# A bias table's 128-fold copy made from DRAM rows in the first MLP instead of from on-chip rows in the first mixer, and a new order of the first loads

## The chip, the cores and the metric

One of the eight cores of a Trainium2 chip runs the whole kernel; the other seven are not used. The metric is the device time of one execution in microseconds (us), as the median of several runs of the same program. Lower is better. Beside these runs one execution was recorded by the hardware profiler, and every row below is from that one.

## The reference

The model is a stack of six layers over 256 tokens of width 1024, in float32, batch 1. Cut to what matters here:

```
x = x                                    # 256 x 1024
for i in 0..3:                           # "first block"
    h = rms_norm(x, norm_mix[i])
    m = retention | conformer | stick_breaking | retention   (h)
    x = x + m
    x = x + (relu(rms_norm(x, norm_ffn[i]) @ w1[i]) ** 2) @ w2[i]      # 1024 -> 4096 -> 1024
x = rms_norm(x, final_norm)
for layer in 0..1:                       # "second block"
    x = hybrid_layer(x, ..., rel_bias)   # short conv + pooling + windowed attention, then a gated MLP
return rms_norm(x, g_final)
```

Windowed attention adds to each score a bias that depends on the head and on key position minus query position: `bias = rel_bias[t5_bucket(rel)]`, 16 heads, `rel_bias` is 32 x 16. So for each head there is one vector over the relative position, and every query row uses the same vector shifted by one.

All weights together are some 400 MB of float32, each read once. With 256 tokens this gives TensorE enough work per byte to be the bound, since each product is taken as three float32r matmuls (high x high, high x low, low x high parts).

## The kernel before

**Units.** All weights lie in one DRAM tensor in the order of use, cut into units of 2 MB (some of 1 MB). A unit is two pieces of 128 x 2048 floats. For each piece: SP (SyncE) issues one DMA into `raw[u % 2]` (L495, `load`, called in loops from `loads` and `mlp`), ScalarE copies it to float32r as the high part `w_hi` (L1113), VectorE subtracts to get the low part `w_lo` (L1512), and TensorE multiplies (L691, L692, L693). There are two slots of each. The load of unit u waits until the low part of unit u-2 is made; the split of unit u waits until TensorE is through with the same piece of unit u-2. `ahead(v)` on ScalarE and VectorE emits the splits up to unit v at that place of the engine's order.

**Order.** Every engine has its own instruction list, written out by hand, and they meet at semaphores only. Nothing is scheduled by a planner. Layer 1 is a retention mixer of 16 units, then an MLP of 16 units (`mlp_walk`), then the conformer, and so on. `row` and `Fori` only fold repeated units into hardware loops.

**The first norm (`norm`, `norm_half`).** It runs in two halves of 128 tokens. For each half ScalarE squares x and sums (L1180), VectorE adds epsilon and inverts (L1576, L1577), ScalarE takes the root (L1183), VectorE scales (L1633), TensorE transposes (L728), VectorE multiplies by the norm's gain, which lies in `cols` (L1639), and ScalarE and VectorE make high and low parts (L1162, L1565). Before the first unit can start, all this must be done for half 0 and both parts of the unit's first piece must be there. At the start SP issues the loads of x half 0, the identity matrix (for transposes), `cols` (the column tables), x half 1, and then the weights. GpSimd (POOL) issues at the same time the tables of the retention mixer (rope, gains, decay), `rel_bias` and the one-hot bucket table. VectorE and TensorE wait for `loaded` to reach 32, which is identity and `cols` both.

**The bias table.** In the first mixer TensorE makes the 16 vectors by one small product (L832), VectorE copies them from PSUM to `B_VEC`, 16 partitions of 512 floats. GpSimd then writes them to a DRAM tensor `scratch` of 16 x 128 x 512 floats (4 MB), each row 128 times. It does so in four DMAs of 1 MB (`store_bias`, L558), each of four heads, thus from four partitions of `B_VEC`, one after each head's rows of the group norm (`ret_gn_w`, `ret_gn_b`, fetched by L537). Much later the two hybrid layers read `scratch` with a row length of 511, which gives each query row its shifted vector. After the first mixer GpSimd fetches a row, zeroes, waits for all four stores (`stored` 64), since its next work overwrites `B_VEC`, and then makes the conformer's diagonal matrices (L583), which TensorE reads in the second layer.

Of the kernel before, what the change touches and what calls it, by code (L numbers as in the profile page):

```python
# [24 lines left out]
F32 = mybir.dt.float32  # L25
F32R = mybir.dt.float32r
ALU = mybir.AluOpType
ACT = mybir.ActivationFunctionType
AX = mybir.AxisListType

P = 128
# [10 lines left out]
N_HEADS, N_KV, HEAD_DIM, WINDOW = 16, 4, 64, 128  # L42
# [269 lines left out]
    last()  # L312

def build_program(nc, stream, columns, x_in, rows, tables, rel_bias, scratch, out):
    col_at, n_cols = column_layout()
    widths = unit_widths()
    n_units = len(widths)
# [3 lines left out]
    with ctx:  # L322
# [3 lines left out]
        def sem(name):  # L326
            return ctx.enter_context(nc.semaphore(name))
# [66 lines left out]
        sca = sem("sca")  # L394
        x_in_place = [sem(f"x_in_place{a}") for a in range(2)]
        loaded = sem("loaded")
        table = sem("table")
        gn_rows = sem("gn_rows")
        bias_in = [sem(f"bias_in{i}") for i in range(2)]
# [21 lines left out]
        def tiles(ap, t=SEQ):  # L421
            return ap.rearrange("p (k t) -> p k t", t=t)
# [57 lines left out]
        @block.sync  # L480
        def _(sp):
            S = Place()

            def load():

                slot, n = S.u % 2, widths[S.u] // 2
                if S.u >= 2:
                    sp.wait_ge(lo_done, S.at(2 * (S.u - 1), "u", 2))
                for piece in range(2):
                    rows_n = P * n // D  # L490
                    row = S.at(S.row, "row")
                    src = stream[row:row + rows_n, :] if S.it is None else stream[bass.ds(row, rows_n), :]
                    if n > D:
                        src = src.rearrange("(p a) n -> p (a n)", p=P)
                    sp.dma_start(raw[slot][:, place_of(S.u, piece)], src).then_inc(arrived[slot][piece], 16)  # L495
                    S.row += rows_n
                S.u += 1

            def loads(n):

                def body():
                    load()
                    load()
                if S.u == 0:
                    body()
                    n -= 2
                repeat(sp, S, n // 2, {"u": 2, "row": 2 * P * UNIT // D}, body)
                if n % 2:
                    load()

            def mlp(chunks, width):
                def step(first):
                    load()
                    load()
                mlp_walk(sp, S, chunks, {"u": 4, "row": 2 * P * (UNIT + width) // D}, load, step, load)

            sp.dma_start(x[:, 0, :], x_in[0:P, :]).then_inc(x_in_place[0], 16)
            sp.dma_start(ident[:], tables["identity"]).then_inc(loaded, 16)
            sp.dma_start(cols[:], columns).then_inc(loaded, 16)
            sp.dma_start(x[:, 1, :], x_in[P:SEQ, :]).then_inc(x_in_place[1], 16)  # L520
            for mixer_units in (16, 6, 8, 16):
                loads(mixer_units)
                mlp(FFN1_CHUNKS, UNIT)
            for layer in range(2):
                loads(14)
                load()
                loads(9)
                mlp(FFN2_CHUNKS, UNIT // 2)
            assert S.row == stream.shape[0] and S.u == n_units
# [3 lines left out]
        def _(pool):  # L533
            S = Place()

            def fetch(dst, src, done=table):
                pool.dma_start(dst, src).then_inc(done, 16)  # L537

            def row_of(src):
                return src.partition_broadcast(P)  # L540
# [6 lines left out]
            def region_free():  # L547

                pool.wait_ge(released, S.due("released"))
# [1 line left out]
            zero(B_REL)  # L551
            zero(B_REL[32:33, :], 1.0)

            def store_bias(part):

                hs = slice(4 * part, 4 * part + 4)
                pool.dma_start(scratch[hs], B_VEC[hs, :].unsqueeze(1).broadcast_to([4, P, 512])).then_inc(stored, 16)  # L558

            def retention(j):  # L560
                if j:
                    region_free()
                fetch(work[:, 5632:6144], tables["rope"])
                fetch(R_GAIN[:, 0, :], row_of(rows["ret_q_norm"][j, :]))
                fetch(R_GAIN[:, 1, :], row_of(rows["ret_k_norm"][j, :]))
                fetch(work[:, 4096:5632], tables["decay"])
                if j == 0:
                    fetch(B_REL[0:32, 0:N_HEADS], rel_bias)
                    fetch(B_HOT, tables["bucket_hot"])
                for h in range(RET_HEADS):  # L570
                    if h:
                        region_free()
                    fetch(R_GN[:, 0, :], row_of(rows["ret_gn_w"][j, RET_DV * h:RET_DV * (h + 1)]), gn_rows)
                    fetch(R_GN[:, 1, :], row_of(rows["ret_gn_b"][j, RET_DV * h:RET_DV * (h + 1)]), gn_rows)
                    if j == 0:
                        if h == 0:
                            pool.wait_ge(bias_vec, 1)
                        store_bias(h)

            def diagonals(n):  # L580

# [17 lines left out]
            fetch(C_B, row_of(rows["conv_pw2_b"][0, :]))  # L599
            zero(C_U[:, :, 0:TAPS - 1])  # L600
            zero(C_MEAN, 1.0 / D)
            pool.wait_ge(stored, 64)
            pool.wait_ge(loaded, 32)
            diagonals(0)
            diagonals(1)
            split_low(CONV_FIRST + 3)
# [12 lines left out]
            retention(1)  # L619
            region_free()  # L620
            fetch(ROW, row_of(rows["final_norm"]), row_in)
            flat = scratch.rearrange("h t r -> h (t r)")
            for layer in range(2):
                if layer:
# [22 lines left out]
            for a in range(2):  # L647
                pool.wait_ge(x_ready, x_signals - 2 + 2 * a)
                pool.dma_start(out[P * a:P * (a + 1), :], xs[:, a, :]).then_inc(stored, 16)
            pool.wait_ge(stored, 96)  # L650

        @block.tensor
        def _(pe):
# [426 lines left out]
                    await_chunks(1)  # L1081
                    unit_r(act_hi, act_lo, 4 * i, 4, i == 0, i == 1)

            pe.wait_ge(loaded, 32)
            first_half()
            for i, mixer in enumerate((retention, conformer, stick_breaking, retention)):
                if i in (0, 3):
# [15 lines left out]
        def _(act):  # L1103
# [81 lines left out]
            def norm(first=False, row=False):  # L1185

                if not first:
                    ahead(S.u)
                for a in range(2):
                    if row:  # L1190
                        norm_half(a)
                    norm_half(a, first)
                    if a == 1:
                        ahead(S.u)
                    use(False)
                    S.v += 1
                    act.wait_ge(value_ready, S.v)
                    for g in range(2):
                        if g == 1:
                            await_drained(S.p - 1)  # L1200
                        round_chunk(act_hi[:, four(g), P * a:P * (a + 1)],
                                    tiles(val[:, g, 512 * a:512 * (a + 1)], P))

            def mlp1():
                def make(ahead_too):
# [190 lines left out]
            def hybrid(layer):  # L1396
# [86 lines left out]
                    round_chunk(act_hi[:, four(i), :], tiles(H_MERGED[:, i, :]))  # L1483
                S.u += 2

            for i, mixer in enumerate((retention, conformer, stick_breaking, retention)):
                norm(first=i == 0)
                mixer()
                norm()
                mlp1()  # L1490
# [12 lines left out]
        def _(dve):  # L1503
# [94 lines left out]
            def inverse_rms(a):  # L1598
                dve.wait_ge(ss_ready, S.due("ss_ready"))
                inverse(rinv[:, a:a + 1], ss[:, a:a + 1])  # L1600
# [9 lines left out]
            def norm(name, add=True, row=False):  # L1610

                if add:
                    ahead(S.u)

                def low(a, g):
                    ts_, cs = slice(P * a, P * (a + 1)), slice(512 * a, 512 * (a + 1))
                    rest_chunk(act_hi[:, four(g), ts_], act_lo[:, four(g), ts_], tiles(val[:, g, cs], P))

                for a in range(2):  # L1620
                    if a == 1:
                        low(0, 0)
                    if add:
                        residual_half(a)
                    elif a == 1:
                        dve.wait_ge(x_in_place[1], 16)
                    if row:
                        row_norm_half(a, x)
                    if a == 1:
                        low(0, 1)  # L1630
                    inverse_rms(a)
                    await_roots()
                    ts(xs[:, a, :], x[:, a, :], rstd[:, a:a + 1], None, ALU.mult).then_inc(xs_ready, 1)  # L1633
                    if not add and a == 1:
                        ahead(S.u)
                    o, done = fetch_pair()
                    S.v += 1
                    for g in range(2):
                        tt(tiles(val[:, g, 512 * a:512 * (a + 1)], P), tiles(o[:, 512 * g:512 * (g + 1)], P),  # L1639
                           by_tile(name, 4 * g, 4, P), ALU.mult).then_inc(done if g else value_ready, 1)  # L1640
                low(1, 0)
                low(1, 1)
# [443 lines left out]
                    rest_chunk(act_hi[:, four(i), :], act_lo[:, four(i), :], tiles(H_MERGED[:, i, :]))  # L2086
                S.u += 2

            dve.wait_ge(loaded, 32)
            dve.wait_ge(x_in_place[0], 16)  # L2090
            for i, mixer in enumerate((retention, conformer, stick_breaking, retention)):
                norm(f"norm_mix{i}", add=i > 0)
# [42 lines left out]
```

## Time and profile before

| | us |
|---|---|
| median of 3 runs | 2608.0 |
| lowest, highest | 2607.62, 2610.07 |
| profiled execution, first to last instruction (span) | 2603.1 |
| TensorE busy in it | 2426.9 (93%) |
| VectorE, ScalarE, GpSimd busy | 1531.0 (59%), 1139.3 (44%), 184.8 (7%) |
| share of the chain that ended last: TensorE, VectorE, DMA, ScalarE | 78%, 11%, 5%, 3% |

The profiled execution is read from its first to its last instruction. Its own time is not listed among the runs; the median of the runs is 4.9 us longer than its span, which is launch and end. TensorE's busy share is an average over a long, even part and a few stretches where it stands still. The first mixer lies between 20 and 251 us of the span, the first MLP between 251 and 444 us, and the second retention mixer, which has the same units and none of the bias table's work, between 1126 and 1335 us.

### The profile page before, as it was taken

Reading aid. Unit: us, or ns where it says so; the run is one execution under the profiler, and the core shown is the slowest. Engines: PE = TensorE matmul, PEld = TensorE weight load, DVE = VectorE, ACT = ScalarE, POOL = GpSimd, SP = SyncE. Lnnn points to the kernel's source line nnn. Section 1 sums busy time; section 2 is a strip of 40 time slices with the busy share of each in tenths; the row PEclk is TensorE's granted clock in tenths of the full one; section 3 lists DMA queues with packets and bytes.
Section 4 is the critical chain, followed back from the end, with each engine's and each line's share of the span. In section 5 each row is a group of like instructions: output and inputs, shape, how many; then the busy total and the mean of one; then the engine's idle time right before and its main releaser. Section 6 shows DMA issues by size and latency. Waiting matters only on the chain.

```text
span 2603.1 us, 35299 instructions
## 1 busy us (share of the span) xinstructions
PE 2426.9 (93%) x14772; PEld 2165.5 (83%) x14772; DVE 1531.0 (59%) x1476; ACT 1139.3 (44%) x1119; POOL 184.8 (7%) x198
## 2 busy tenths in 40 slices
PE   7988899859999899999999999997999999979998
PEld 5766898848997789977879979996899899968997
DVE  6655555986556664476664566457654564485544
ACT  5433444224445843354443444354444433453443
POOL 0000810611000000000000000002000000020000
PEclk9999999989999999999999999998999999989999
DMA  6565444213444245434454435351444444522443
GB/s 237 161 178 162 182 181 181 98 65 130 181 184 175 82 158 194 193 151 181 178 199 194 193 130 194 147 205 57 176 166 189 185 184 169 187 105 114 169 179 128
DMA packets 68402, 424.35 MB, mean 163 GB/s; under 512 B 10832, under 2 KB 11120, under 8 KB 22464
## 3 DMA queue, kind: packets, MB, share of 16 engines
q1 hardware_dynamic: 58752, 399.83, 40.0%
q0 software_dynamic: 9536, 22.87, 3.8%
q8 instruction: 87, 1.43, 0.2%
q14 instruction: 27, 0.22, 0.0%
HBM read 417.40 MB, written 5.24 MB: 162 GB/s over the span
## 4 chain that ended last, share of the span: by engine, by line
PE 78%; DVE 11%; DMA 5%; ACT 3%; issue 2%; SPq 0%; POOL 0%; DVEq 0%; ACTq 0%; POOLq 0%
PE pair L691 16%; PE pair L693 16%; PE pair L692 16%; PE acc L691 8%; PE acc L692 8%; PE acc L693 8%; DMA raw<-weights 3%; DVE work L1812 2%; DVE work L1792 2%; DMA work<-ret_gn_b 1%; DVE w_lo L1512 1%; PE pair L728 1%; PE pair L1056 1%; ACT work L1180 1%; DVE work L2036 1%
## 5 line engine op out<-in xcount | busy, mean ns | idle before, releaser
L1512 DVE TENSOR_TENSOR w_lo<-raw,w_hi 128x2048 fp32r<-128x2048 f32 (+1 forms) x394 | 837.8, 2159 | 312.6 <-ACT w_hi L1113 311.8
L1113 ACT ACTIVATE w_hi<-raw 128x2048 fp32r<-128x2048 f32 (+1 forms) x404 | 713.7, 1805 | 214.7 <-PE acc L693 133.4
L691 PE MATMUL pair<-act_hi,w_hi 128*128 128x256 f32 x2496 | 708.7, 284 | 3.1 <-DVE w_lo L1512 3.1
L693 PE MATMUL pair<-act_hi,w_lo 128*128 128x256 f32 x2496 | 706.3, 283 | 0.0
L692 PE MATMUL pair<-act_lo,w_hi 128*128 128x256 f32 x2496 | 706.3, 283 | 0.0
L691 PEld LDWEIGHTS pair<-act_hi,w_hi 128*128 128x128 f32 x2496 | 478.9, 192 | 6.1 <-issue 3.8
L692 PEld LDWEIGHTS pair<-act_lo,w_hi 128*128 128x128 f32 x2496 | 478.9, 192 | 2.3
L693 PEld LDWEIGHTS pair<-act_hi,w_lo 128*128 128x128 f32 x2496 | 478.9, 192 | 0.0
L691 PE MATMUL acc<-w_hi,hid_hi 128*128 128x512 f32 x848 | 336.2, 397 | 10.8 <-DVE hid_lo L1565 10.8
L692 PE MATMUL acc<-w_lo,hid_hi 128*128 128x512 f32 x848 | 332.4, 392 | 0.0
L693 PE MATMUL acc<-w_hi,hid_lo 128*128 128x512 f32 x848 | 331.9, 391 | 0.0
L691 PE MATMUL pair<-w_hi,act_hi 128*128 128x512 f32 (+1 forms) x576 | 226.2, 393 | 13.1 <-DVE w_lo L1512 7.9
L693 PE MATMUL pair<-w_hi,act_lo 128*128 128x512 f32 (+1 forms) x576 | 222.3, 386 | 0.0
L692 PE MATMUL pair<-w_lo,act_hi 128*128 128x512 f32 (+1 forms) x576 | 222.3, 386 | 0.0
L691 PEld LDWEIGHTS acc<-w_hi,hid_hi 128*128 128x128 f32 x848 | 160.7, 190 | 44.8 <-DVE hid_lo L1565 11.6
L693 PEld LDWEIGHTS acc<-w_hi,hid_lo 128*128 128x128 f32 x848 | 160.3, 189 | 34.0
L692 PEld LDWEIGHTS acc<-w_lo,hid_hi 128*128 128x128 f32 x848 | 160.7, 190 | 32.8 <-issue 1.4
L1654 DVE TENSOR_TENSOR val<-gate 128x1024 f32<-128x1024 f32 x32 | 39.2, 1225 | 207.7 <-ACT gate L1207 207.7
L691 PEld LDWEIGHTS pair<-w_hi,act_hi 128*128 128x128 f32 x576 | 109.3, 190 | 39.0 <-issue 11.5
L1207 ACT ACTIVATE gate<-pair 128x1024 f32<-128x1024 f32 x32 | 32.8, 1026 | 243.2 <-PE pair L693 237.2
L693 PEld LDWEIGHTS pair<-w_hi,act_lo 128*128 128x128 f32 x576 | 109.1, 189 | 21.9
L692 PEld LDWEIGHTS pair<-w_lo,act_hi 128*128 128x128 f32 x576 | 109.2, 190 | 21.2 <-issue 0.7
(209 smaller groups left out, 2683.7 us busy)
## 6 DMA issues: line engine op xcount, KB each, us to landing
raw<-weights SPq DMA_DIRECT2D x356, 1024.0 KB, 6.7
raw<-weights SPq DMA_DIRECT2D x48, 512.0 KB, 6.4
work<-bias_scratch POOLq DMA_DIRECT2D x32, 192.0 KB, 3.4
bias_scratch<-work POOLq DMA_DIRECT2D x4, 1024.0 KB, 48.4
work<-ret_gn_w POOLq DMA_DIRECT2D x8, 256.0 KB, 5.0
work<-ret_gn_b POOLq DMA_DIRECT2D x8, 256.0 KB, 12.7
work<-table_pool POOLq DMA_DIRECT2D x2, 1024.0 KB, 5.6
work<-table_decay POOLq DMA_DIRECT2D x2, 768.0 KB, 8.9
```

The lines of the kernel that those rows point to most:

```text
L691: mm(o, a_hi, b_hi, start=start, stop=False)
L692: mm(o, a_hi, b_lo, start=False, stop=False)
L693: return mm(o, a_lo, b_hi, start=False, stop=stop)
L728: last = tr(o[:, P * k:P * (k + 1)], xs[:, a, P * k:P * (k + 1)], ident[:])
L1056: last = mm(o[:, 512 * i:512 * i + SEQ], H_V[:, s, P * (j // 4):P * (j // 4) + P], H_PT[:, j % 2, i, s, :], start=s == 0, stop=s == 1)
L1113: run(w_hi[slot][:, part], raw[slot][:, part], ACT.Copy).then_inc(hi_done, 1)
L1180: run(xs[:, a, :], x[:, a, :], ACT.Square, scale=D ** -0.5, accum_out=ss[:, a:a + 1]).then_inc(ss_ready, 1)
L1207: run(gate[:, slot, :], o[:], ACT.Relu).then_inc(done, 1)
L1512: tt(w_lo[slot][:, part], raw[slot][:, part], w_hi[slot][:, part].bitcast(F32), ALU.subtract).then_inc(lo_done, 1)
L1654: tt(val[:, S.c % 2, :], gate[:, slot, :], gate[:, slot, :], ALU.mult).then_inc(value_ready, 1)
L1792: ins = stt(C_Y[:, k, :], C_U[:, k, m:m + SEQ], colv("dw_w", KT * m + k), C_Y[:, k, :], ALU.mult, ALU.add)
L1812: ins = stt(dst, src, w, dst, ALU.mult, ALU.add)
```

## The change

The bias vectors are stored once, as 16 rows, to a new DRAM tensor `bias_rows` (one DMA of 32 KB). The four DMAs that make 128 copies read those rows from DRAM, and GpSimd issues them together once the first mixer is over. GpSimd waits only for the small store before that, and for all four copies only before the hybrid layers. The loads at the start get another order: the first unit of weights is issued piece by piece around x half 1, GpSimd's tables wait until the first unit has landed (`arrived[0][1]`), the wait for `cols` moves to the instruction that reads it, ScalarE's root table is loaded ahead by a dummy root, and on ScalarE and VectorE the split of the first unit stands ahead of the second half's norm. Note that `load()` issues both pieces of a unit; so the order on SP is x half 0, identity, `cols`, unit 0, x half 1, unit 1.

```diff
@@ SP
-                if S.u == 0:
-                    body()
-                    n -= 2
...
             sp.dma_start(x[:, 0, :], x_in[0:P, :]).then_inc(x_in_place[0], 16)
             sp.dma_start(ident[:], tables["identity"]).then_inc(loaded, 16)
-            sp.dma_start(cols[:], columns).then_inc(loaded, 16)
+            sp.dma_start(cols[:], columns).then_inc(cols_in, 16)
+            load()
             sp.dma_start(x[:, 1, :], x_in[P:SEQ, :]).then_inc(x_in_place[1], 16)
-            for mixer_units in (16, 6, 8, 16):
+            load()
+            for mixer_units in (14, 6, 8, 16):
@@ GpSimd
-            def store_bias(part):
-                hs = slice(4 * part, 4 * part + 4)
-                pool.dma_start(scratch[hs], B_VEC[hs, :].unsqueeze(1).broadcast_to([4, P, 512])).then_inc(stored, 16)
             def retention(j):
                 if j:
                     region_free()
+                else:
+                    pool.wait_ge(arrived[0][1], 16)
                 fetch(work[:, 5632:6144], tables["rope"])
...
-                    if j == 0:
-                        if h == 0:
-                            pool.wait_ge(bias_vec, 1)
-                        store_bias(h)
+                    if j == 0 and h == 0:
+                        pool.wait_ge(bias_vec, 1)
+                        pool.dma_start(bias_rows, B_VEC[0:N_HEADS, :]).then_inc(stored, 16)
...
             zero(C_MEAN, 1.0 / D)
-            pool.wait_ge(stored, 64)
-            pool.wait_ge(loaded, 32)
+            pool.wait_ge(stored, 16)
+            for part in range(4):
+                hs = slice(4 * part, 4 * part + 4)
+                pool.dma_start(scratch[hs], bias_rows[hs].unsqueeze(1).broadcast_to([4, P, 512])).then_inc(stored, 16)
+            pool.wait_ge(loaded, 16)
+            pool.wait_ge(cols_in, 16)
             diagonals(0)
...
             fetch(ROW, row_of(rows["final_norm"]), row_in)
+            pool.wait_ge(stored, 80)
@@ TensorE
-            pe.wait_ge(loaded, 32)
+            pe.wait_ge(loaded, 16)
             first_half()
@@ ScalarE, norm
                     norm_half(a, first)
-                    if a == 1:
+                    if a == 1 and not first:
                         ahead(S.u)
...
+                    if a == 0 and first:
+                        ahead(S.u)
@@ ScalarE, start
+            act.wait_ge(root_primed, 1)
+            run(small[:, 127:128], small[:, 126:127], ACT.Sqrt)
@@ VectorE, norm
-                    elif a == 1:
-                        dve.wait_ge(x_in_place[1], 16)
...
                     if a == 1:
                         low(0, 1)
+                        if not add:
+                            ahead(S.u)
+                            dve.wait_ge(x_in_place[1], 16)
                     inverse_rms(a)
                     await_roots()
                     ts(xs[:, a, :], x[:, a, :], rstd[:, a:a + 1], None, ALU.mult).then_inc(xs_ready, 1)
-                    if not add and a == 1:
-                        ahead(S.u)
                     o, done = fetch_pair()
+                    if not add and a == 0:
+                        dve.wait_ge(cols_in, 16)
@@ VectorE, start
-            dve.wait_ge(loaded, 32)
+            nc.vector.memset(small[:, 126:127], 1.0).then_inc(root_primed, 1)
             dve.wait_ge(x_in_place[0], 16)
```

## Rows read from the trace of the kernel before

**Rows 1.** Page: the span, and the shares of the chain that ended last.

```profile
span 2603.1 us, 35299 instructions
...
PE 78%; DVE 11%; DMA 5%; ACT 3%; issue 2%; SPq 0%; POOL 0%; DVEq 0%; ACTq 0%; POOLq 0%
```

**Rows 2.** Busy time by stretch: mixers, MLPs, an even part, a part at half clock.

```profile
core 0: us, PE busy (x) PEld busy (x) DVE busy (x) ACT busy (x) POOL busy (x), PEclk, DMA share, GB/s
85.23:251.29 166.06, 145.89 (x619) 115.89 (x619) 90.39 (x86) 64.12 (x48) 6.65 (x9) 0.94 0.61 169
1191.46:1335.12 143.66, 139.77 (x619) 111.51 (x619) 89.75 (x85) 63.50 (x48) 3.21 (x6) 1.00 0.48 177
251.29:444.14 192.85, 185.44 (x1132) 165.79 (x1130) 101.12 (x65) 80.88 (x59) 63.47 (x65) 0.98 0.51 190
608.94:792.19 183.25, 182.32 (x1131) 163.92 (x1130) 100.56 (x65) 80.68 (x59) 6.55 (x8) 1.00 0.48 184
...
340.00:420.00 80.00, 80.00 (x524) 73.61 (x523) 40.52 (x21) 30.55 (x20) 0.00 (x0) 1.00 0.51 197
158.20:168.40 10.20, 5.33 (x15) 4.39 (x16) 5.61 (x5) 5.62 (x4) 0.00 (x0) 0.50 0.46 137
```

**Rows 3.** TensorE's waits, 0 to 300 us: total, times, longest.

```profile
PE pair L854 <- ACT work L1263: 12.3, 3, 8.6
...
PE acc L691 <- DVE hid_lo L1565: 8.3, 2, 5.9
```

**Rows 4.** Chain of waits, 85 to 300 us: start, length, what.

```profile
93.61 31.46 DMA raw<-weights
...
130.05 30.12 DMA raw<-weights
...
249.26 28.42 DMA raw<-weights
```

**Rows 5.** Landing of the weights' DMAs, issues of 260 to 440 us.

```profile
DMA to landing us min/median/max: 4.7/6.6/8.9
```

**Rows 6.** Page, DMA issues: count, size of each, median us to landing.

```profile
bias_scratch<-work POOLq DMA_DIRECT2D x4, 1024.0 KB, 48.4
```

**Rows 7.** Timeline of ScalarE, VectorE and TensorE, 0 to 21 us, in parts.

```profile
4.08 1.06 ACT L1180 ACTIVATE work<-x 128x1024 f32<-128x1024 f32 x1 [2.04 <-DMA x<-x_in]
5.05 0.19 ACT L1180 ACTIVATION_READ_ACCUMULATOR work<-x 128x1 f32 x1
5.25 1.28 ACT L1183 ACT_TABLE_LOAD   x1
...
8.68 0.15 DVE L1576 TENSOR_SCALAR small<-small 128x1 f32<-128x1 f32 x1 [8.68 <-DMA cols<-columns]
...
12.90 1.22 ACT L1162 ACTIVATE act_hi<-val 128x512 fp32r<-128x512 f32 x2 [3.63 <-DVE val L1639]
...
15.69 1.89 ACT L1113 ACTIVATE w_hi<-raw 128x2048 fp32r<-128x2048 f32 x1
17.62 2.29 DVE L1512 TENSOR_TENSOR w_lo<-raw,w_hi 128x2048 fp32r<-128x2048 f32 x1 [1.05 <-ACT w_hi L1113]
...
20.06 0.77 PE L691 MATMUL pair<-w_hi,act_hi 128*128 128x512 f32 x1 [7.92 <-DVE w_lo L1512]
```

**Rows 8.** DMA from 82.5 to 85 us: the first store alone.

```profile
DMA packets 795, 0.07 MB, mean 27 GB/s; under 512 B 780, under 2 KB 780, under 8 KB 795
```

**Rows 9.** DMA from 2594 to 2597 us: one output store; packets, MB, engine share.

```profile
q0 software_dynamic: 144, 0.52, 43.1%
```

**Rows 10.** GpSimd: the last store's issue and the diagonals behind the wait.

```profile
226.04 1.12 POOL L558 DMA_DIRECT2D bias_scratch<-work  x1 [32.75 <-issue]
...
274.33 62.41 POOL L583 TENSOR_SCALAR work<-ident,cols 128x128 f32<-128x128 f32 x62 [11.59 <-issue]
```

**Rows 11.** Waits of ScalarE, 608 to 792 us: its splits wait on TensorE.

```profile
ACT w_hi L1113 <- PE acc L693: 24.6, 7, 3.5
```

**Rows 12.** DMA from 18 to 23 us: all kinds together.

```profile
DMA packets 315, 1.90 MB, mean 380 GB/s; under 512 B 48, under 2 KB 48, under 8 KB 118
```

More of the change, by code:

```diff
@@ L312, in mlp_walk, with build_program @@
     last()
-def build_program(nc, stream, columns, x_in, rows, tables, rel_bias, scratch, out):
+def build_program(nc, stream, columns, x_in, rows, tables, rel_bias, bias_rows, scratch, out):
     col_at, n_cols = column_layout()
@@ L396, in build_program @@
         loaded = sem("loaded")
+        cols_in = sem("cols_in")
+        root_primed = sem("root_primed")
         table = sem("table")
@@ L649, in _ @@
                 pool.dma_start(out[P * a:P * (a + 1), :], xs[:, a, :]).then_inc(stored, 16)
-            pool.wait_ge(stored, 96)
+            pool.wait_ge(stored, 112)
         @block.tensor
@@ L2128 @@
     tables = {k: given("table_" + k, v) for k, v in constant_tables().items()}
+    bias_rows = nc.dram_tensor("bias_rows", (N_HEADS, 512), F32).ap()
     scratch = nc.dram_tensor("bias_scratch", (N_HEADS, P, 512), F32).ap()
@@ L2131 @@
     build_program(nc, given("weights", lay_out_weights(a)), given("columns", lay_out_columns(a)),
-                  given("x_in", a["x"][0]), rows, tables, given("rel_bias", a["rel_bias_2"]), scratch, out)
+                  given("x_in", a["x"][0]), rows, tables, given("rel_bias", a["rel_bias_2"]), bias_rows, scratch,
+                  out)
     result = run_bass_kernel_spmd(nc, [arrays], core_ids=[0])
```

## The prediction

> **What bounds the kernel now.** I read the page first. The chain that ended last is TensorE for 78% [rows 1], so a change pays only where TensorE stands still or runs at the lower clock. The page has no such place by name, so I read the first layer by stretches against later layers with the same units. Retention mixer 0 from its first attention product (85.23 us) to the next norm takes 166.06 us; the same stretch of retention mixer 1, with the same 619 matmuls, takes 143.66 us [rows 2]. The first MLP takes 192.85 us, the second, with the same 1132 matmuls, 183.25 us [rows 2]. So 22.4 us and 9.6 us are lost there to something that later layers don't have. TensorE's waits show it standing for ScalarE and VectorE results, 12.3 us and 8.3 us, with single waits of 8.6 and 5.9 us [rows 3]. Their causes stand in the chain of waits: behind them are loads of weights that need 28.4 to 31.5 us to land [rows 4], where 6.6 us is usual [rows 5]. Each of these lies beside one store of the bias table, which takes 48.4 us [rows 6]. After such a wait the clock is at its lower level, 1.2 GHz, for some 10 us (158.2 to 168.4 us, granted clock 0.50 [rows 2]). At the opening TensorE's first product of a unit starts at 20.06 us, released by the low part of the weights [rows 7].
>
> **Why a store is slow.** Alone on the queues it moves 27 GB/s [rows 8]. One output store from 128 partitions moves 0.52 MB in 43.1% of 16 engines for 3 us, which is 20.7 engine-us, so 25.3 GB/s for each engine [rows 9]. The store of four partitions thus gets about one engine's rate in all, while the weights on the same engines queue behind it: in the chain, four pieces of 1 MB are out at once and the last needs about 30 us, 7.5 us each, or 15.0 us for a unit. The MLP wants a unit each 183.25 / 16 = 11.45 us. That gives the stall: 48.4 x (1 - 11.45 / 15.0) = 11.5 us at most per store, less what is buffered; measured are (22.4 + 9.6) / 4 = 8.0 us, lower clock included.
>
> **The change, part by part.**
>
> *Four stores leave mixer 0.* Only one store of 32 KB remains, a thirty-second of one of the four. The stretch becomes that of mixer 1: 166.06 - 143.66 = 22.4 us gained. Nothing else differs after 85 us; the group norm's rows are fetched in both. Bounds: 20 (a late landing remains) to 22.4.
>
> *The first MLP loses its share of the fourth store,* issued at 226.04 and over by 274.33, where GpSimd goes on behind its wait for it [rows 10]: 192.85 - 183.25 = 9.6 us gained.
>
> *Four copies DRAM to DRAM enter the first MLP.* The trace has none such, so I bound it. From below: 4.2 MB at 25.3 GB/s per engine [rows 9] over 16 engines is 10.4 us of DMA time. The DMA share there is 0.51 at 197 GB/s [rows 2], so half of the engines' time is free, and the copies are through in some 20 us. A weight packet of 8 KB takes 8.2 / (197 / 0.51 / 16) = 0.34 us of an engine, a copy's 4 KB 0.16 us; if an engine takes one of each in turn, a piece (8 packets per engine) needs 4.0 us and a unit 8.0 us, below the 11.45 wanted. It makes no difference to this whether the four copies use four engines each or all use the same four. ScalarE's splits wait on TensorE in an MLP, not on DMAs [rows 11], so a landing some us later is hidden. From above: each copy costs what a store costs now or more (rivals below). Below nothing is excluded, since the work is added. I take 0.5 us, near the lower end, since the nearest rows with a spread source or target [rows 9] show full rate and only the four-partition source shows 27 GB/s.
>
> *GpSimd.* Its four issues of 1.12 us [rows 10] come ahead of the diagonals, and the wait for the stores goes. Now the diagonals start at 274.33 and take 62.4 us [rows 10], and they are read after 444 us. They may be 100 us late at no cost. The wait for the copies now stands before the hybrid layers, two mixers and three MLPs on.
>
> *The opening,* step by step. ScalarE squares half 0 from 4.08 and has the sum at 5.24 [rows 7]. VectorE goes on only at 8.68, when `cols` has landed. With that wait moved it starts at 5.27, so 3.41 us earlier. The root's table load (5.25 to 6.53) was hidden by that wait; now it would cost 0.9 us, and the dummy root moves it ahead of 4.08, in an idle time of 2.04 us that ended with x. `cols` itself, needed 3.5 us after the start of L1576, lands at 8.65 or earlier, as the tables of GpSimd no longer share the engines: just in time. So the first high part of the activations moves from 12.90 to 9.49 and the pair of them ends at 10.71. Then ScalarE splits the weights at once, instead of after half 1's square and root: from 15.69 to 10.73, gain 4.96. VectorE's low part follows 1.93 us later and TensorE 2.44 us after that [rows 7]: 15.10 instead of 20.06. Condition: the first piece is there at 10.73. It is behind `cols` (8.65 at the latest) and takes 1.05 MB / 380 GB/s [rows 12] = 2.8 us, so 11.4 at the latest; earlier if `cols` is. Half 1's chain moves behind the splits, but ends near 19 us, and TensorE turns it only after 15 products, near 21 us. The tables that now wait for the first unit (about 12.5 us) are 1.5 MB of some 4.5 MB queued then, all landed by 12.5 + 4.5 / 0.38 = 24.3; VectorE wants them near 25. The first products run at the lower clock; after a stall that lasts up to 10 us [rows 2], and if it lasts a few us longer here than it did, up to 1.9 us go. I take 4.5 us; bounds 2.6 and 5.0.
>
> **Sum.** 22.4 + 9.6 + 4.5 - 0.5 = 36.0 us. The span goes from 2603.1 to 2567.1; the runs' median lies 4.9 us above the span, so 2608.0 becomes 2572.0. All later layers shift as they are, since their chains start at the end of the first MLP.
>
> **The rivals.**
>
> *R1, the copies stay slow but run side by side.* If it is the 2 KB rows or the writes into DRAM that set the rate, and not the source's partitions, each copy still takes 48 us, and the four together load all 16 engines for that time. One stretch of 11.5 us of stall, plus some 2 us at the lower clock: 13.5 in place of 0.5, 2585. For it: the rows of the store don't separate source from target. Against it: the 27 GB/s is just one engine's rate. The Trainium skill (DMA: Bandwidth & Descriptors, "Rules for kernel authors") says that an outermost dimension of size c below 16 confines a DMA to at most c engines, and the copies still have 4 outermost, so it speaks for narrow copies. With narrow copies at full engine rate the sum stays; with slow ones it is R1 or R2, and no row before shows which.
>
> *R2, slower than before.* The copies stay slow and queue one after another on the same four engines: 4 x 48.4 = 194 us, the whole MLP. Then every unit takes 15.0 instead of 11.45 us: 16 x 3.55 = 57 us lost against 36.5 gained, 2628. It decides from 11.45 + 36.5 / 16 = 13.7 us per unit on. The weights' 30 us landings [rows 4] speak for it, the wide stores' rate [rows 9] against it.
>
> *R3, the stalls only move:* each copy costs 8.0 us in the MLP as each store does now, 32 in all, and only the opening stays: 2603.5.
>
> *R4, the opening gives nothing,* since the first weights or `cols` come late under the saturated queues (380 GB/s [rows 12]): 2576.5.
>
> **Chances.** Forecast 0.72, R1 0.12, R4 0.09, R3 0.04, R2 0.03. What can be told from no change is about 0.2%, 5.2 us. Faster: 0.72 + 0.12 + 0.09 = 0.93; within it R3, 0.04; slower R2, 0.03. The range reaches from 2568 us (all terms at their upper bound and a us or two of clock) to 2585, R1's value, where about 1 in 10 is left above.
>
> **What would show it.** The mixer from its first attention product to the next norm takes 143 to 146 us, and no weights' load needs over 15 us. The first MLP takes 183 to 185 us; each copy lands in under 30 us, and the clock stays at 1.00 between 30 us and the end of this MLP. The first product of a unit starts near 15 us. The forecast is wrong if TensorE waits for `hid_lo` or a split in the first MLP with a weights' load behind it (R1 to R3), or if L1113 waits for a DMA near 11 us (R4).

## The result and the profile after

The changed kernel takes 2569.93 us (median of 4 runs, 2568.25 to 2571.21) against 2607.81 us (4 runs, 2606.49 to 2610.07) beside it: 37.9 us less, ratio 0.9852, 95% interval 0.984 to 0.9864. The forecast was 2572.0 us, with a range of 2568 to 2585 and a chance of 0.93 that the kernel gets faster. In the profiled executions the span fell by 34.1 us only, from 2603.1 to 2569.0; the difference is explained below.

The page of the changed kernel: the span, the shares of the chain that ended last, the landing of the copies.

```profile
span 2569.0 us, 35304 instructions
...
PE 86%; DVE 10%; ACT 3%; issue 1%; DMA 0%; POOL 0%; DVEq 0%; ACTq 0%
...
bias_scratch<-bias_rows POOLq DMA_DIRECT2D x4, 1024.0 KB, 22.7
```

DMA had 5% of the chain [rows 1] and has 0% now. By stretches (length, busy time of each engine, granted clock, DMA share, GB/s): head, mixer 0, mixer 1, first MLP, second MLP.

```profile
15.16:79.55 64.39, 62.45 (x283) 50.71 (x283) 52.21 (x67) 36.22 (x61) 2.28 (x5) 1.00 0.53 207
79.55:223.98 144.43, 141.26 (x619) 112.66 (x619) 89.92 (x86) 63.48 (x48) 3.23 (x6) 0.99 0.48 180
1155.70:1300.13 144.43, 141.26 (x619) 112.62 (x619) 89.85 (x85) 63.45 (x48) 3.22 (x6) 0.99 0.48 178
223.98:407.20 183.22, 182.29 (x1131) 163.91 (x1129) 100.96 (x65) 80.69 (x59) 62.61 (x69) 1.00 0.56 212
574.32:757.53 183.21, 182.25 (x1131) 163.91 (x1130) 100.55 (x65) 80.69 (x59) 6.60 (x8) 1.00 0.48 184
```

These answer [rows 2]. Mixer 0 went from 166.06 to 144.43 us and is now as long as mixer 1 to a hundredth. The first MLP went from 192.85 to 183.22 us, the length of every other, although 4 MB of copies (DMA at 212 instead of 184 GB/s) run in it.

The opening, ScalarE, VectorE and TensorE, answers [rows 7]: start, length, what, and what ended the idle time before.

```profile
0.77 1.28 ACT L1491 ACT_TABLE_LOAD   x1 [0.77 <-PEq L2121]
4.17 1.06 ACT L1182 ACTIVATE work<-x 128x1024 f32<-128x1024 f32 x1 [1.91 <-DMA x<-x_in]
5.83 0.20 ACT L1185 ACTIVATE small<-small 128x1 f32<-128x1 f32 x1 [0.51 <-DVE small L1583]
9.66 1.23 ACT L1164 ACTIVATE act_hi<-val 128x512 fp32r<-128x512 f32 x2 [3.63 <-DVE val L1646]
10.80 3.69 ACT L1115 ACTIVATE w_hi<-raw 128x2048 fp32r<-128x2048 f32 x2
...
5.44 0.15 DVE L1582 TENSOR_SCALAR small<-small 128x1 f32<-128x1 f32 x1 [4.54 <-ACT work L1182]
...
15.16 0.77 PE L693 MATMUL pair<-w_hi,act_hi 128*128 128x512 f32 x1 [6.26 <-DVE w_lo L1518]
```

The first product starts at 15.16 instead of 20.06 us. ScalarE takes both pieces of the first unit with no wait for a load: the first piece lands at 9.36 us, where it landed at 14.84 us before.

GpSimd's timeline, which answers [rows 10]:

```profile
75.51 0.51 POOL L575 DMA_DIRECT2D bias_rows<-work  x1 [58.58 <-DVE work L1730]
...
236.13 1.12 POOL L602 DMA_DIRECT2D bias_scratch<-bias_rows  x1 [0.73 <-POOL work L545]
259.68 1.10 POOL L602 DMA_DIRECT2D bias_scratch<-bias_rows  x1 [22.43 <-issue]
283.52 1.09 POOL L602 DMA_DIRECT2D bias_scratch<-bias_rows  x1 [22.74 <-issue]
306.05 1.08 POOL L602 DMA_DIRECT2D bias_scratch<-bias_rows  x1 [21.43 <-issue]
307.25 57.17 POOL L580 TENSOR_SCALAR work<-ident,cols 128x128 f32<-128x128 f32 x62
```

Here the forecast's picture was off: the copies don't go out together. Each is issued 0.3 to 0.4 us after the one before has landed, so they fill 92 us and not 20, and the diagonals start 33 us later than before, in spite of a mixer that ends 27 us earlier. They still end 43 us ahead of the end of the MLP. The trace of before showed the same: its stores were issued at 81.22, 127.57, 176.96 and 226.04 us, the last three 0.35 to 0.42 us after the one before had landed. The sign in [rows 10] is the 32.75 us that GpSimd stood idle before the last store, with nothing that the profile shows to wait for. So a store was under way almost without a break from 81 to 274 us.

One stretch shows how copy and weights share an engine. From 254 to 258 us DMA's share is 0.27, some four of 16 engines, so only the engines that the copy uses are at work:

```profile
254.00:258.00 4.00, 4.00 (x20) 3.30 (x19) 3.59 (x3) 4.00 (x4) 0.00 (x0) 1.00 0.27 109
```

109 GB/s over 4.3 engines is 25 GB/s for each, the rate of the output store [rows 9]. In this stretch the trace has 34 copy packets of 4 KB, of 0.159 us, and 34 weight packets of 8 KB, of 0.309 us: one of each in turn, as the sum assumed (0.16 and 0.34 us). The slowest weight load took 12.6 us (min/median/max 4.7/6.7/12.6), and no split waited for one.

### The profile page after: what moved, and what is told of

It is laid out like the page before. It is cut to its first block, busy times and chain, and to the rows that moved or that the text cites. A ratio compares the mean times of both kernels' runs of the same rounds, so it can differ in the third digit from the quotient of the medians.

```text
span 2569.0 us, 35304 instructions
## 1 busy us (share of the span) xinstructions
PE 2421.5 (94%) x14772; PEld 2162.4 (84%) x14772; DVE 1530.4 (60%) x1477; ACT 1137.2 (44%) x1119; POOL 180.5 (7%) x199
## 4 chain that ended last, share of the span: by engine, by line
PE 86%; DVE 10%; ACT 3%; issue 1%; DMA 0%; POOL 0%; DVEq 0%; ACTq 0%
PE pair L693 18%; PE pair L695 17%; PE pair L694 17%; PE acc L693 9%; PE acc L694 9%; PE acc L695 9%; DVE work L1819 2%; DVE work L1799 2%; PE pair L730 1%; PE pair L1058 1%; PE acc L1037 1%; ACT work L1182 1%; PE pair L1000 1%; DVE work L2043 1%; ACT act_hi L1164 0%
## 5 line engine op out<-in xcount | busy, mean ns | idle before, releaser
L695 PEld LDWEIGHTS acc<-w_hi,hid_lo 128*128 128x128 f32 x848 | 160.0, 189 | 34.1
## 6 DMA issues: line engine op xcount, KB each, us to landing
bias_scratch<-bias_rows POOLq DMA_DIRECT2D x4, 1024.0 KB, 22.7
```

The costliest lines, as they stand in the source:

```text
L695: return mm(o, a_lo, b_hi, start=False, stop=stop)
```

## The experiments

All times are against the kernel before on the same chip. Stretches are those of [rows 2]: the mixer from its first attention product to the next norm, then the first MLP.

### The opening alone, and the copies alone

`e_open_only` has the diff's edits of the opening and the four old stores; `e_copies_only` has the diff's copies and the old opening (its first product comes at 20.65 us).

> Kernel before with the new opening alone; the four stores stay in mixer 0. Main theory (the parts add up): first product of a unit near 15.2 us instead of 20.06, the mixer stretch from the first attention product to the next norm stays near 166 us and the first MLP near 192.9 us, time about 4.9 us below before. Rival (the stalls beside the stores absorb a head start, since they end when weights land): the mixer stretch grows by the 4.9 us, time within 1 us of before.

> Kernel before with the bias rows stored once and the four DRAM-to-DRAM copies in the first MLP; the opening as before. Main theory: first product at 20 us, mixer stretch 144 us, first MLP 183 us, time 31 to 33 us below before; the copies follow one another and land in 22 to 24 us each. Rival (the copies only fit because the new opening gives a lead): first MLP above 186 us.

The opening alone takes 2603.69 us (11 runs) against 2607.58 (15 runs), ratio 0.9982 (0.9973 to 0.9991). Mixer and MLP, of `e_open_only` and then of `e_copies_only`:

```profile
79.71:247.95 168.24, 148.54 (x619) 117.75 (x619) 90.42 (x86) 64.12 (x48) 6.64 (x9) 0.92 0.59 168
247.95:439.45 191.50, 184.12 (x1131) 164.90 (x1130) 101.38 (x65) 80.89 (x59) 66.12 (x65) 0.99 0.51 191
```

```profile
84.91:229.34 144.43, 141.27 (x618) 112.64 (x619) 89.95 (x86) 63.49 (x48) 3.23 (x6) 0.99 0.49 180
229.34:412.56 183.22, 182.28 (x1131) 163.91 (x1130) 101.07 (x65) 80.67 (x59) 62.74 (x69) 1.00 0.56 212
```

The first product of `e_open_only` comes at 15.16 us, and 4.7 of the 4.9 us are there still at the end of the first MLP (439.45 against 444.14). The mixer is 2.2 us longer, the MLP 1.4 shorter. So the stalls do not absorb the head start, though the mixer takes 2.2 us of it for a while. The copies alone give 2575.96 us, ratio 0.9879 (0.9864 to 0.9894), 31.6 us less, with both stretches as in the changed kernel. The parts add up: 31.6 + 3.9 = 35.5 us against 37.9 for both, within the spread of the runs.

### Source or place

Two kernels with the old opening separate what the change does in one step. `e_dram_in_mixer` takes the copies from DRAM rows but at the old places:

```diff
-                    if j == 0 and h == 0:
-                        pool.wait_ge(bias_vec, 1)
-                        pool.dma_start(bias_rows, B_VEC[0:N_HEADS, :]).then_inc(stored, 16)
+                    if j == 0:
+                        if h == 0:
+                            ...
+                            pool.wait_ge(stored, 16)
+                        hs = slice(4 * h, 4 * h + 4)
+                        pool.dma_start(scratch[hs], bias_rows[hs].unsqueeze(1).broadcast_to([4, P, 512])).then_inc(stored, 16)
```

> Opening as before; the rows go once to DRAM and the four 1 MB copies from DRAM are issued at the old four places in mixer 0. Main theory (the source counts: four partitions give one engine's rate, DRAM rows don't): mixer stretch 144 to 147 us, first MLP 183 to 184 us, copies land in 15 to 24 us, time 30 to 33 us below before. Rival (the place counts: the mixer has no slack for a 1 MB copy, the MLP has): mixer stretch 152 us or more, time at most 22 us below before.

`e_sbuf_in_mlp` keeps the on-chip source but issues at the new place:

```diff
-                pool.dma_start(scratch[hs], bias_rows[hs].unsqueeze(1).broadcast_to([4, P, 512])).then_inc(stored, 16)
+                pool.dma_start(scratch[hs], B_VEC[hs, :].unsqueeze(1).broadcast_to([4, P, 512])).then_inc(stored, 16)
...
             diagonals(0)
+            pool.wait_ge(stored, 64)
```

> Opening as before; the four stores keep their on-chip source of four partitions but are issued in the first MLP, one after another. GpSimd must wait for them before the second set of diagonals, so these come late and the conformer may wait for them; the verdict is read from the MLP. Main theory (source counts): mixer stretch 144 us, and the first MLP has a stall beside every store: 192.9 - 183.2 is what most of one store costs, so four of them give 200 to 240 us (15.0 us per unit over all 16 units would be 240). Rival (place counts): first MLP 183 to 187 us.

Mixer and MLP of `e_dram_in_mixer`, then of `e_sbuf_in_mlp`, and three loads of the latter from its chain of waits (start, length):

```profile
87.30:230.99 143.69, 139.79 (x619) 111.53 (x619) 89.84 (x86) 63.46 (x48) 6.66 (x9) 1.00 0.58 206
230.99:414.21 183.22, 182.28 (x1132) 163.93 (x1130) 101.35 (x65) 80.69 (x59) 73.84 (x65) 1.00 0.49 193
```

```profile
85.59:229.25 143.66, 139.75 (x619) 111.52 (x619) 89.86 (x86) 63.49 (x48) 3.20 (x6) 1.00 0.48 179
229.25:452.32 223.07, 193.01 (x1132) 171.18 (x1130) 101.19 (x65) 82.05 (x59) 48.00 (x51) 0.92 0.57 170
```

```profile
253.17 31.46 DMA raw<-weights
289.67 27.66 DMA raw<-weights
...
353.25 31.70 DMA raw<-weights
```

DRAM rows in the mixer cost nothing: 143.69 us, copies land in 22.9 us, 2576.41 us in all, ratio 0.9877 (0.9862 to 0.9893), the same as `e_copies_only`. The on-chip rows in the MLP cost 223.07 - 183.22 = 39.9 us there. TensorE stands for them in two kinds of wait for a split, and the rest is mostly its clock: busy time is 193.01 us instead of 182.28 for the same products, at a granted clock of 0.92.

```profile
PE acc L689 <- DVE w_lo L1510: 16.8, 3, 9.7
PE pair L689 <- DVE w_lo L1510: 11.5, 2, 9.2
```

So 28.3 us are waits and 10.7 us the lower clock. The kernel takes 2615.68 us against 2608.44, ratio 1.0033 (1.0023 to 1.0044), slower than before. So the source gives the whole gain and the place none. With the old source, moving to the MLP alone is a loss.

### The width of the copy

`e_wide_sbuf` changes only which part of the table one store writes. Place, source tensor and bytes stay as before:

```diff
-                hs = slice(4 * part, 4 * part + 4)
-                pool.dma_start(scratch[hs], B_VEC[hs, :].unsqueeze(1).broadcast_to([4, P, 512])).then_inc(stored, 16)
+                ts_ = slice(32 * part, 32 * part + 32)
+                pool.dma_start(scratch[:, ts_, :], B_VEC[0:N_HEADS, :].unsqueeze(1).broadcast_to([N_HEADS, 32, 512])).then_inc(stored, 16)
```

> Kernel before, stores at the old places in mixer 0 and still from on-chip rows, but each store writes 32 copies of all 16 rows, so its source is 16 partitions instead of 4. Opening as before. If the source's partitions set the rate (four ports of 27 GB/s, by the Trainium skill, SBUF - State Buffer, Door 1): a store lands in 12 to 14 us instead of 48, mixer stretch 144 to 148 us, time 28 to 33 us below before. Rival (an on-chip source to DRAM in 2 KB rows is slow as such, 27 GB/s for the DMA): landing stays near 48 us and, with all 16 engines behind it, the mixer stretch is 166 us or more.

Mixer and MLP, and the landing of its four stores:

```profile
84.54:228.25 143.71, 139.81 (x619) 111.51 (x619) 89.86 (x86) 63.49 (x48) 5.13 (x9) 1.00 0.67 207
228.25:411.47 183.22, 182.28 (x1132) 163.92 (x1130) 101.31 (x65) 80.69 (x59) 73.59 (x65) 1.00 0.48 190
```

```profile
DMA to landing us min/median/max: 12.0/12.7/13.3
```

A store from 16 partitions lands in 12.7 us, and one from four in 48.4 [rows 6]. The time is 2576.71 us, ratio 0.9882 (0.9867 to 0.9897): the copies' whole gain, with no detour through DRAM. The Trainium skill (SBUF — State Buffer, "Door 1: The DMA port swizzle") gives 104 GB/s as measured for partitions 0 to 15 and 1 MiB. By that figure a store would take 10.1 us, an estimate; the 12.7 us here, beside weights' loads, are somewhat above it.

This kernel changes two things at once, the partitions of the source and the number of engines, and its time alone doesn't separate them. The DRAM copies do in part: with four outermost they land in 22.7 us, so four engines alone don't make a store last 48.4 us. The packets settle the rest. In `e_sbuf_in_mlp` a store's packet of 4 KB takes 0.34 us when two of them are under way at once, 0.48 us with three and 0.62 us with four (medians), while a DRAM copy's packet takes 0.16 us with any number from one to four. So the four engines of a store share one rate of some 4 x 4.1 / 0.62 = 26 GB/s, and it isn't that each partition has a fixed low rate of its own, which would give 0.6 us at any number. With 16 packets from 16 partitions under way (`e_wide_sbuf`) one takes 0.61 us, which is 107 GB/s in all, four times as much. The same times say why weights are late. Averaged over what is under way, a store's packet takes 0.51 us in `e_sbuf_in_mlp` and 0.60 us in the kernel before (84 to 106 and 229 to 260 us). An engine that takes one packet of each kind in turn, as was counted for the copies, would then need 0.82 to 0.91 us for every weight packet, thus 6.6 to 7.3 us for the eight packets of a piece, near the 7.5 that the forecast read from the landings.

`e_wide_dram` does the same to the changed kernel's copies (`bias_rows.unsqueeze(1).broadcast_to([N_HEADS, 32, 512])`), and `e_half_copies` cuts each into two of 64 copies, still four heads each.

> Changed kernel, but each of the four copies writes 32 copies of all 16 rows, so the outermost dimension is 16 and not 4. By the Trainium skill (DMA: Bandwidth & Descriptors, Rules for kernel authors) a copy then uses 16 engines instead of 4: it lands in 4 to 8 us instead of 22.7, and GpSimd issues the next one that much sooner, so the diagonals start some 60 us earlier. Time the same as the changed kernel within 1 us, since the first MLP is already at 183.2. Rival (GpSimd's issue gaps of 22 us have another cause, and the DRAM rows' rate sets the landing): landing stays above 15 us. Second rival: wide copies hit all weights' engines at once and the first MLP goes above 185 us.

> Changed kernel, but each of the four copies is cut in two of 64 copies each, still with 4 outermost. In the changed kernel GpSimd issued a copy only when the one before had landed (gaps of 22 us), in the wide version all four without a gap. If the issue waits for room on the few engines that a narrow copy uses (the same four each time), then the first two or more halves go out at once, and the gaps that follow are about half as long, 10 to 12 us each; all eight are out near 306 us as before. Rival (GpSimd lets only one narrow copy be under way at a time, whatever its size): every half waits for the one before, eight gaps of 10 to 12 us. Second rival (they use different engines and only the number of descriptors in one DMA counts): no gaps at all, all out by 242 us. In each case the first MLP stays at 183.2 us.

GpSimd's timeline, of the wide and then of the half copies:

```profile
236.31 2.57 POOL L602 DMA_DIRECT2D bias_scratch<-bias_rows  x4 [0.31 <-POOL work L545]
239.00 69.33 POOL L580 TENSOR_SCALAR work<-ident,cols 128x128 f32<-128x128 f32 x62
```

```profile
235.98 2.65 POOL L602 DMA_DIRECT2D bias_scratch<-bias_rows  x3 [0.38 <-POOL work L545]
256.97 2.49 POOL L602 DMA_DIRECT2D bias_scratch<-bias_rows  x3 [18.34 <-issue]
278.13 1.65 POOL L602 DMA_DIRECT2D bias_scratch<-bias_rows  x2 [18.67 <-issue]
279.90 40.42 POOL L580 TENSOR_SCALAR work<-ident,cols 128x128 f32<-128x128 f32 x42
```

All four wide copies go out in 2.6 us, and the last lands at 262.3 us, so all 4 MB take 26 us from the first issue. (The four count on one semaphore, so the landings of the first three can't be told apart for certain.) The diagonals start 68 us earlier. The slowest weights' load takes 15.0 us and ScalarE waits 1.9 us for one, but TensorE does not: the MLP takes 183.23 us, and the time is 2570.79 us against 2608.44, ratio 0.9858 (0.9842 to 0.9874), as the changed kernel. I had expected each copy to land in 4 to 8 us, which overlooked that they would now share the engines with each other.

The halves go out three at a time, which is none of the three patterns I had written down: the first theory had "two or more at once" right, its gaps (18 us for 10 to 12) and its end (279 us for 306) wrong. Its premise, that narrow copies use the same four engines each time, is wrong too. From 238.5 to 243 us the trace has 4, then 8, then 12 packets of the halves under way at once, so three halves use three groups of four engines; under one copy of the changed kernel it is at most four but for some 3% of the time. A theory of room for rows on one engine therefore doesn't fit as it stood. Shown is only this: one copy of 1 MB with 4 outermost, three halves, or all four wide copies go out together, and the next group follows 0.4 us after the last of the group has landed (256.58 and 277.78 us). What limits the group stays open. The MLP takes 183.22 us again, and the time is 2569.79 us in one run.

### The opening, piece by piece

Five variants of the changed kernel, each with one thing altered. `e_tables_first` takes away GpSimd's wait for the first unit; `e_no_prime` the dummy root; `e_cols_wait` puts the wait for `cols` back ahead of the first norm; `e_late_split` puts `ahead(S.u)` back behind the second half's root and scaling; `e_piece_early` (with the wide copies) puts the first piece's split between the two activation chunks:

```diff
+                        if first and a == 0:
+                            split_piece(0, g)
+                            S.split = g
```

> Changed kernel without GpSimd's wait for the first unit, so its tables load from 1.5 us on as before. If the order of the loads carries the opening: the first piece lands after 12 us instead of near 9.4, L1115 waits for a DMA and the first product comes at 17 us or later. Rival (the first pieces land in time anyway and only the order of the engines' instructions counts): first product within 0.3 us of 15.16.

> Changed kernel without the dummy root. Main theory: the root's table loads after the sum of half 0, from about 5.3 to 6.6 us, so the root comes at 6.6 instead of 5.83 and the first product near 15.9 to 16.0 instead of 15.16. Rival (another table is loaded once anyway and the start is set by the weights): 15.16 within 0.2.

> Changed kernel, but VectorE waits for the column tables before the first norm, as before. The tables land near 6.9 us now (before: 8.65). Main theory: L1582 starts near 6.9 instead of 5.44, and the first product comes 1.3 to 1.7 us later than 15.16 (16.5 to 16.9). Rival (the weights' split is the last to be ready whatever VectorE does): 15.16 within 0.3.

> Changed kernel, but ScalarE and VectorE split the first unit after half 1's norm, as before. Main theory: half 1's square and root stand ahead of the split, so the first product comes 1.5 to 2.0 us later than 15.16 (16.7 to 17.2), or later if half 1 of x, now behind the first unit in the queue, lands after 11 us: then up to 18.6. Rival (loads alone carry the opening): 15.16 within 0.3.

> As e_wide_dram, and in the opening ScalarE and VectorE take the first piece's split between the two activation chunks of half 0. Expected: first product at 14.5 to 14.8 us instead of 15.16, 0.4 to 0.6 us less in all, which only the timeline can tell. Rival: the first piece has not landed near 10.3 us and the start stays at 15.1 or later.

TensorE's first product in `e_tables_first`, `e_no_prime`, `e_cols_wait`, `e_late_split` and `e_piece_early`, from their timelines:

```profile
15.15 0.77 PE L691 MATMUL pair<-w_hi,act_hi 128*128 128x512 f32 x1 [6.28 <-DVE w_lo L1516]
```

```profile
15.96 0.76 PE L693 MATMUL pair<-w_hi,act_hi 128*128 128x512 f32 x1 [6.26 <-DVE w_lo L1516]
```

```profile
16.65 0.77 PE L693 MATMUL pair<-w_hi,act_hi 128*128 128x512 f32 x1 [6.26 <-DVE w_lo L1518]
```

```profile
12.82 1.06 ACT L1182 ACTIVATE work<-x 128x1024 f32<-128x1024 f32 x1 [1.86 <-DMA x<-x_in]
...
18.93 0.76 PE L693 MATMUL pair<-w_hi,act_hi 128*128 128x512 f32 x1 [9.96 <-DVE w_lo L1516]
```

```profile
14.71 0.76 PE L693 MATMUL pair<-w_hi,act_hi 128*128 128x512 f32 x1 [5.67 <-DVE w_lo L1519]
```

So at the first product the opening's parts are worth 0.8 us (dummy root), 1.5 us (wait for `cols`), 3.8 us (split ahead of half 1), and nothing for the tables' delay. The last was a miss: with the tables under way the first piece landed at 10.75 us instead of 9.36, just in time for the split at 10.77; only the second piece and half 1 came late (ScalarE waited 2.39 us for the piece). TensorE's first attention product came at 80.04 us, between the 79.55 of the changed kernel and the 80.88 of `e_wide_dram`, which has the same opening, so no loss shows there either. The other half of the new load order, the first unit ahead of half 1 of x, was not tried by itself. It can't be free: with both halves of the old order the first piece landed at 14.84 us, 4.1 us after the 10.7 at which ScalarE now takes it. One run each gave 2571.40 us without the tables' delay, 2570.76 without the dummy root, 2571.19 with the wait for `cols` and 2573.11 with the late split, too close together for one run to rank them. `e_late_split` is above its range, since half 1 of x is now behind the first unit in the queue: ScalarE waited 1.86 us for it, and the weights' split behind that. The parts don't add, for each later step waits for the latest of its inputs. `e_piece_early` starts 0.45 us sooner, as expected, and takes 2570.79 us against 2608.44, ratio 0.9856 (0.984 to 0.9873). No version here beats the changed kernel by more than the spread of the runs.

## Why the prediction was right

**The stores were the first layer's loss.** Forecast 22.4 and 9.6 us; measured in the trace 21.63 and 9.63. TensorE's waits of up to 8.6 us [rows 3] are gone, and so are ScalarE's for weights. Of the 22.4 us, 0.8 is missing, because the clock was at its lower level from 213.0 to 216.4 us, after TensorE had stood 2.4 us at the end of the mixer (granted 0.99 for the whole mixer instead of 1.00). So the sign that the clock stays at 1.00 up to the end of the MLP did not hold. Mixer 1 shows the same in this execution, and `e_dram_in_mixer` has 143.69 with the clock at 1.00.

**The four-partition source was the cause.** The step held: the source-or-place pair shows the source, and the packets' times show that the four engines share one rate. This also answers R1 and R2: the copies' writes into DRAM in 2 KB rows take 0.16 us per 4 KB, so it is not they that are slow. R2 was right that the copies follow one another, which the forecast's "in some 20 us" had not, and wrong that they are slow. With the old source, the pile of stores in the MLP gives 39.9 us of loss. The rival's 57 was too large, since it took 15.0 us for all 16 units; the prediction's own 11.5 us per store would give 46 us at most for four, and what is buffered comes off that. R3 took 8.0 us per store; moved into the MLP each costs 10.0 us. That the MLP wants its units faster than the mixer is a likely reason, not a shown one.

**The copies cost 0.5 us: measured 0.0.** The one-for-one sharing held in the stretch that was counted, 34 packets of each kind. Wrong was "through in some 20 us": they follow one another and take 92 us. It was harmless for the reason given in the forecast, that an engine which takes one packet of each kind in turn still delivers weights faster than the MLP wants them; the wide version shows the other end, also at 183.2 us.

**The opening: 4.5 us.** The chain gave 15.10 and the trace has 15.16 us, so 4.9 us sooner. The allowance for the clock was not needed in this execution, where the head was even 0.78 us shorter (64.39 against 65.17 from the first product to the first attention product); that part is luck, for `e_wide_dram` with the same opening has 65.66. Alone the opening is worth 3.9 us by the medians (4.7 by the ratio, 2.3 to 7.0). R4 fell.

**The sum.** Up to the end of the first MLP the trace shows 444.14 - 407.20 = 36.9 us, where the forecast had 36.0. The rest of the program was to shift unchanged, and in these two executions it took 2.9 us more (2158.9 and 2161.8 us). Most of it is the conformer:

```profile
407.20:574.32 167.12, 125.91 (x677) 109.69 (x676) 134.53 (x199) 46.64 (x51) 48.89 (x37) 0.88 0.21 78
```

The kernel before had 164.80 us there at a granted clock of 0.90. All twelve experiments have 166.2 to 168.4 us, and `e_open_only`, which keeps the old stores, has 166.60. So 164.80 is what one quick execution had and no effect of the change.

**What the sum doesn't hold: the spread of the executions.** The table ahead of the prediction takes the 4.9 us between the profiled span of before and the runs' median for launch and end. That is wrong. The changed kernel's profiled execution is one of its runs, and there the gap is 1.75 us (2570.75 against a span of 2569.0). So the profiled execution of before would have been a run of about 2604.9, at the lower end of 2604.50 to 2611.06 over 15 runs and 3.0 us below its median, and the changed kernel's was 0.8 us above its own. Hence 34.1 us by the two spans and 37.9 by the medians. The forecast took its 36.0 us off a median, so the wrong 4.9 cancels in it. By the interval of the ratio the gain is 35.5 to 41.7 us, and the 36.0 lies within. The 2569.93 itself is below what the terms can give, for at their upper bounds they add up to 37.0 us, thus 2571.0; only the allowance of a us or two in the range covers it.

## What to carry to other kernels

When a small transfer takes long, divide its bytes by its time and compare with one engine's rate before moving it. Here 27 GB/s pointed to the four partitions of the source, and another slice of the same table (16 partitions for 32 copies) gave the same gain as the detour through DRAM and the new place. A load is late only if its landing outlasts the buffers, so look for weights' loads that need several times their usual time, and for what lies beside them on the same engines.

At a program's start, follow the chain that releases the first product. The order of instructions on the engines that prepare it counts, each wait on a tensor should stand at its first reader, and the first weights must have landed by then. Here this was worth 4.9 us at the first product and 3.9 us of the run, and delaying the other tables nothing.

## What I had not expected

GpSimd doesn't issue a 1 MB copy with four outermost while another is under way. There are gaps of 22 us between the copies, and of 45 to 48 us between the old stores in `e_sbuf_in_mlp`, while with 16 outermost all four go out in 2.6 us. It costs nothing here, but whatever stands behind such DMAs on GpSimd is late by their landing.

A head start doesn't carry through to the microsecond. `e_cols_wait` starts its first product 1.5 us after the changed kernel's, and its span is 2569.4 against 2569.0 us; `e_no_prime` starts 0.8 us later with a span of 2569.0. These are one execution each. Mixer stretches with identical work are 143.65 to 143.71 us in some executions (clock 1.00) and 144.43 us in others (0.99), and the conformer goes with them or against them. A change of under some 2 us is better read in its own stretch than in the total.
